# A different division of work between VectorE, ScalarE and GpSimd at three norms and in one attention of a fused transformer kernel

## What is computed

```python
h = _modulate(_rms_norm(x, g), shift, scale)     # h * (1 + scale) + shift
x = x + gate * _rms_norm(h_after_the_matrices, g_post)
```

```python
s = q . k * scale + mask            # 128 queries see themselves and up to 128 keys back
p = exp(s - max) / (sum(exp(s - max)) + exp(sink - max))
o = p . v
```

## Time and profile before

| | |
|---|---|
| median of 3 runs | 1689.22 us (1688.07 to 1692.46) |
| the profiled execution | 1697.89 us, of which the span is 1696.1 us |
| PE, PE weight load | 92% and 78% of the span |
| VectorE, ScalarE, GpSimd | 58%, 54% and 4% |
| norms that the diff touches | at about 366 to 384, 749 to 767 and 982 to 991 us of the span |
| the second attention | at about 1543 to 1625 us |

### The profile page before, as it was taken

One profiled execution on the slowest core, in us unless ns is written; L12 is line 12 of the kernel. 1 busy time (PEld: TensorE's weight loads), 2 busy tenths in 40 slices (PEclk: granted clock), 3 DMA queues, 4 the chain that ended last, 5 costly groups with the idle time before them and its releaser, 6 DMA issues.

```text
span 1696.1 us, 25703 instructions
## 1 busy us (share of the span) xinstructions
PE 1564.8 (92%) x10227; PEld 1315.7 (78%) x10227; DVE 984.4 (58%) x1602; ACT 918.0 (54%) x1518; POOL 63.3 (4%) x82
## 2 busy tenths in 40 slices
PE   5999898979999999979989989998999999888887
PEld 3777555748788888848845889998999999888777
DVE  2463666564343434464754676667766767577655
ACT  5653645464132323455555554556777867376745
POOL 3000032000000000000003000000000000000000
PEclk9999977989999999989986899999999999999899
DMA  7731535342433232342306366663635444343232
GB/s 245 222 99 50 174 100 174 119 129 75 149 100 99 91 102 82 113 143 75 124 13 207 118 197 191 197 199 128 227 127 173 150 150 141 109 133 117 91 108 75
DMA packets 223640, 225.40 MB, mean 133 GB/s; under 512 B 8234, under 2 KB 222064, under 8 KB 223472
## 3 DMA queue, kind: packets, MB, share of 16 engines
q1 hardware_dynamic: 222816, 223.63, 41.1%
q0 software_dynamic: 704, 0.12, 0.0%
HBM read 222.68 MB, written 1.05 MB: 132 GB/s over the span
## 4 chain that ended last, share of the span: by engine, by line
PE 73%; ACT 11%; DVE 11%; issue 2%; POOL 1%; DMA 0%; SPq 0%; DVEq 0%; ACTq 0%; POOLq 0%
PE bank L1039 20%; PE bank L1040 19%; PE bank L1041 19%; ACT SH L1701 2%; PE bank L1075 2%; ACT whi L1565 1%; DVE wlo L2116 1%; PE bank L1327 1%; PE bank L1060 1%; ACT H L1807 1%; PE bank L1234 1%; ACT HH L1807 1%; PE bank L1242 1%; PE bank L1349 1%; PE bank L1394 1%
## 5 line engine op out<-in xcount | busy, mean ns | idle before, releaser
L2116 DVE TENSOR_TENSOR wlo<-raw,whi 128x1024 fp32r<-128x1024 f32 (+2 forms) x322 | 387.9, 1208 | 259.0 <-ACT whi L1565 254.5
L1565 ACT ACTIVATE whi<-raw 128x1024 fp32r<-128x1024 f32 (+2 forms) x322 | 336.0, 1046 | 278.7 <-PE bank L1041 259.1
L1039 PE MATMUL bank<-HH,whi 128*128 128x512 f32 (+2 forms) x640 | 246.2, 385 | 22.1 <-DVE HL L2138 19.3
L1040 PE MATMUL bank<-HL,whi 128*128 128x512 f32 (+2 forms) x640 | 241.9, 378 | 0.0
L1041 PE MATMUL bank<-HH,wlo 128*128 128x512 f32 (+2 forms) x640 | 241.7, 378 | 0.0
L1039 PE MATMUL bank<-HA,whi 128*128 128x256 f32 x576 | 165.4, 287 | 13.7 <-DVE LA L2138 5.2
L1040 PE MATMUL bank<-LA,whi 128*128 128x256 f32 x576 | 162.3, 282 | 0.0
L1041 PE MATMUL bank<-HA,wlo 128*128 128x256 f32 x576 | 162.1, 281 | 0.0
L1039 PEld LDWEIGHTS bank<-HH,whi 128*128 128x128 f32 (+1 forms) x640 | 121.3, 190 | 50.8 <-issue 17.0
L1041 PEld LDWEIGHTS bank<-HH,wlo 128*128 128x128 f32 (+1 forms) x640 | 121.0, 189 | 23.6 <-issue 0.7
L1040 PEld LDWEIGHTS bank<-HL,whi 128*128 128x128 f32 (+1 forms) x640 | 121.5, 190 | 22.9 <-issue 1.2
(11 more groups left out here) (371 smaller groups left out, 3208.1 us busy)
## 6 DMA issues: line engine op xcount, KB each, us to landing
raw<-in_w_ff_dram SPq DMA_DIRECT2D x64, 1024.0 KB, 5.3
raw<-in_w_mod_dram SPq DMA_DIRECT2D x48, 1024.0 KB, 5.2
raw<-in_a_w_in_dram SPq DMA_DIRECT2D x40, 1024.0 KB, 5.0
raw<-in_w_in_dram SPq DMA_DIRECT2D x18, 1024.0 KB, 5.3
raw<-in_b_w_in_dram SPq DMA_DIRECT2D x9, 1024.0 KB, 5.3
raw<-in_w_out_dram SPq DMA_DIRECT2D x8, 1024.0 KB, 5.2
raw<-in_ple_w_gate_dram SPq DMA_DIRECT2D x8, 1024.0 KB, 5.1
raw<-in_a_w_out_dram SPq DMA_DIRECT2D x4, 1024.0 KB, 5.0
```

The costliest lines, as they stand in the source:

```text
L1039: nc.tensor.matmul(o, wh, xh, start=start, stop=False, skip_group_check=shared)
L1040: nc.tensor.matmul(o, wh, xl, start=False, stop=False, skip_group_check=shared)
L1565: f(whi[h % HALF_SLOTS][:, 0:n], raw[u.id % RAW_SLOTS][:, (h % 2) * n:(h % 2) * n + n], ACT.Copy)\
L2116: v.tensor_tensor(wlo[h % HALF_SLOTS][:, 0:n], raw[u.id % RAW_SLOTS][:, (h % 2) * n:(h % 2) * n + n], whi[h % HALF_SLOTS][:, 0:n].bitcast( ...
```

## The change

Four exponentials per pair that VectorE multiplied in `att2_scale` of the second attention are multiplied by GpSimd, as products of two tensors in which the inverse is broadcast along the columns; VectorE stops after the reciprocal and signals it (`s_p_inv`), and the transposes wait for GpSimd's signal (`s_p2_pool`). Layer 0's attention in the second block is as it was.

At the norms a table `h_by_dve` says for which tiles VectorE makes the full value. For 512 tokens these are k = 2, 4 and 6, except at the very first norm, which stays as it was; ScalarE then makes the high part of these tiles by one copy of the full value (128x512), and waits for it. For 256 tokens they are k = 0, 1, 3 and 5, and ScalarE makes the full values of 2, 4, 6 and 7 as well as all high parts.

```diff
+    h_by_dve = {True: (2, 4, 6), False: (0, 1, 3, 5)}
...
-            pe.wait_ge(s_p2, s_p2.at(ip))
+            if i == 0:
+                pe.wait_ge(s_p2, s_p2.at(ip))
+            else:
+                pe.wait_ge(s_p2_pool, s_p2_pool.at(ip))
...
+                first = (l, which) == (0, "mix")
+                by_dve = k in h_by_dve[t == ALL] and not first
+                if by_dve and t == ALL:
+                    act.wait_ge(s_h32, s_h32.at((l, which, k)))
+                    f(hi_part("h", l, which, k, slice(*t)), H32[n][:, k % 2, t[0]:t[1]], ACT.Copy).then_inc(*s_hh.tick((l, which, k)))
+                    continue
                 ops = [(hi_part("h", l, which, k, ts_), ts_, s) for s, ts_ in segs(t)]
-                if t == ALL:
+                if not by_dve:
...
-                if t != ALL:
-                    dve.wait_ge(s_xn, s_xn.at((l, "n", which, a_)))
-                    dve.wait_ge(s_fused, s_fused.at((l, which, a_ // 2)))
-                    for k in range(a_, b_):
-                        ins = v.tensor_scalar(H32[k // 2 % 2][:, k % 2, sl], XN[k // 2 % 2][:, k % 2, sl], fA[:, k, 0:1], modT[l][:, a + k, 0:1],
-                                              ALU.mult, ALU.add)
-                    ins.then_inc(*s_h32.tick(*((l, which, k) for k in range(a_, b_))))
+                for k in range(a_, b_):
+                    if k in by_dve:
+                        dve.wait_ge(s_xn, s_xn.at((l, "n", which, k)))
+                        dve.wait_ge(s_fused, s_fused.at((l, which, k // 2)))
+                        if k >= 4:
+                            dve.wait_ge(s_parts, s_parts.at((l, which, k - 4)))
+                        for s, ts_ in segs(t):
+                            ins = v.tensor_scalar(H32[k // 2 % 2][:, k % 2, ts_], XN[k // 2 % 2][:, k % 2, ts_], fA[:, k, 1 - s:2 - s],
+                                                  modT[l][:, a + k, 1 - s:2 - s], ALU.mult, ALU.add)
+                        ins.then_inc(*s_h32.tick((l, which, k)))
...
             if i == 1:
                 chain(v.tensor_tensor(small[:, total:total + 4], small[:, total:total + 4], small[:, sink:sink + 4], ALU.add))
+                v.reciprocal(small[:, inv:inv + 4], small[:, total:total + 4]).then_inc(*s_p_inv.tick(ip))
+                return
...
+            elif kind == "att2_second" and args[0][0] == 1:
+
+                ip = args[0]
+                pool.wait_ge(s_p_inv, s_p_inv.at(ip))
+                for e in (0, 1):
+                    for part, (a, n) in enumerate(((0, P), (P, SEQ))):
+                        c = att_col(ip, 3, e, part)
+                        p_ = att_p(ip, e)[:, a:a + n]
+                        ins = nc.gpsimd.tensor_tensor(p_, p_, bc(small[:, c:c + 1], [P, n]), ALU.mult)
+                ins.then_inc(*s_p2_pool.tick(ip))
```

More of the change, by code:

```diff
@@ L261, in build @@
     s_p2 = signal("p2")
+    s_p_inv = signal("p_inv")
+    s_p2_pool = signal("p2_pool")
     s_p_hi = signal("p_hi")
@@ L2385, in low @@
                 dve.wait_ge(s_hh, s_hh.at((l, which, b_ - 1)))
-                if t != ALL:
-                    dve.wait_ge(s_h32, s_h32.at((l, which, b_ - 1)))
+                for k in range(a_, b_):
+                    if k in by_dve:
+                        dve.wait_ge(s_h32, s_h32.at((l, which, k)))
                 (hi, lo), t0 = parts("h", l, which)
@@ L2391, in low @@
                      s_parts.tick(*((l, which, k) for k in range(a_, b_))))
+            by_dve = h_by_dve[t == ALL] if (l, which) != (0, "mix") else ()
             groups = [(0, 1), (1, 2), (2, 4), (4, 6), (6, 8)] if ups is None else [(k, k + 1) for k in range(*some)]
```

## The result

The changed kernel takes 1678.75 us (median of 9 executions, 1677.67 to 1684.28) where the kernel before, run beside it, takes 1692.46 (9 executions, 1688.07 to 1696.97). The ratio is 0.9927, with a 95% interval of 0.9912 to 0.9942: 12.4 us less, and 9.8 us at least (the two medians as they stand differ by 13.7). The forecast was 6.3 us less, 1683 us, with a range of 1678 to 1689. The kernel before does not repeat as well as the changed one: it lies between 1687.1 and 1699.1 us in all comparisons, its median was 1692.5, 1694.3, 1690.6 and 1689.9 in the four of them, and its profiled execution, 1697.89, is near the upper end. So the 19.4 us between the two profiled executions are no measure of the change.

The account below looks back on a forecast made before the run. PE, busy 92% of the span, was taken as the bound, so gains come only where it stands still. Terms 2.5 + 1.2 + 0.6 + 2.0 = 6.3 us, off the median of 1689.22: 1683 us, range 1678 to 1689.

Parts of the forecast that it names:

- The norm before layer 0's feed-forward part: Norm of 512 tokens: last low part starts 2.7 us earlier, PE finishes its wait for it 2.5 us earlier.
- The norm before layer 1's mixer: Norm of 512 tokens: PE late only by 0.7 us of the first wait and 0.49 of the last, gain 1.2 us.
- The norm of 256 tokens: VectorE loses four of eight full values, low parts come earlier, ScalarE's later last tile costs nothing: gain 0.6 us.
- The second attention: Chain gains 3.1 us at pairs 0, 1, 2, less 1.3 for locks, plus 0.2 at pair 7: 2.0 us.
- GpSimd's price: Second attention: GpSimd's four products put at 2.5 us a pair, between 2.3 and 4.2.
- the lock: VectorE and GpSimd block each other in the second attention: 0.3 us at each of three pairs, 0.4 once more.
- PE's loss at pair 1: Second attention: PE loses 0.7 us waiting for GpSimd, made up before the next two pairs' scores.
- Pair 7: Second attention: GpSimd's slower products and contention spend nearly all of VectorE's 1.04 us; 0.2 us remain.
- (a): Rival: the second attention gives nothing, locks and late transposes take back its 2.0 us; 1684.9 us, chance 0.22.
- (b): Rival: the norms' gain stays off PE's path, 1 to 2 us left of 4.3; 1686 us, chance 0.13.
- (c): Rival: slower, GpSimd's broadcast products take 4.2 us a pair, change loses from about 3.5; 1695.4 us, chance 0.07.
- (d): Rival: more than forecast, one stretch of low clock goes and pair 7 gains 1.04 us; 1680.5 us, chance 0.13.

Follow-up runs that it names:

- e6: Kernel before with only the norm before layer 1's mixer divided in the new way: 0.9971 of the kernel before, 4.9 us less.
- e12: Changed kernel, but VectorE does the four products itself at pairs 1 and 7 of the second attention: 1681.34 us, 0.9942 of the kernel before.
- e1: Kernel before with only the norms changed, second attention as before: 0.9927 of the kernel before, 12.4 us less.
- e11: Changed kernel measured again beside the kernel before, the second comparison: 1680.63 us beside 1689.94, ratio 0.9942.
- e2: Kernel before with only the second attention changed, all norms as before: 0.9983 of the kernel before, 2.9 us less.
- e4: Changed kernel with GpSimd's products per pair doubled, the added four into a tile nothing reads: 0.9947 of the kernel before.
- e13: As e12, but at norms of 512 tokens VectorE makes full values of tiles 0, 3, 5, 7: 1678.47 us, 0.9928 of the kernel before.
- e8: Kernel before with 14 products left out of layer 1's input projection, 3.2 us less work: 0.9994 of the kernel before, 1.0 us less.
- e9: Kernel before with 14 products done twice in layer 1's input projection, 3.2 us more work: 1.0017 of the kernel before, 2.9 us more.
- e5: Kernel before with only the norm before layer 0's feed-forward part divided in the new way: 0.9969 of the kernel before, 5.3 us less.

## Why the prediction was right, and where it was not

The direction and the mechanism were right: the gains that the traces show lie where PE waited for a low part or where VectorE's queue held the attention back. 1678.75 us lies in the range given, but only 0.75 us above its lower end. The size was too small, 6.3 us for 9.8 and 12.4. Term by term:

**The norm before layer 0's feed-forward part, 2.5 us.** Right. Up to the next norm the traces have 383.3 or 385.0 us before and 381.1 or 382.0 with the change, 2.2 to 3.0 less, and PE takes up the last two tiles 2.5 us earlier. The last low part is at 14.1 us as forecast (13.9 to 14.3), the copy at 0.63 (0.6 to 0.7), ScalarE's two waits at 0.76 and 0.75 (0.7 and 0.6), and the waits of 1.01 and 0.87 us are gone.

**The norm before layer 1's mixer, 1.2 us.** Too small by half; PE takes up the last two tiles 2.5 us earlier and the stage is 2.6 us shorter. The step that failed is "At layer 1 PE was late only by 0.7 of the first wait and by the 0.49 of the last": it took the gain to be what was left of the waits, with PE as slow between them as in that execution. But the last low part set PE's time in both executions of the kernel before, 17.21 us behind ScalarE's first instruction, with a wait of 0.49 in one and 0.85 in the other. e6 begins this norm just as the profiled execution of before did, with a first wait of 6.23 us; its next wait is 1.37 for 1.99, so 1.1 us of idle time are gone, about what the term says. Yet PE's second stretch of lower clock, 3.4 us long and 9.4 us behind ScalarE's first instruction in before, isn't there in e6, and PE takes up the last two tiles at 14.69. So the term kept a stretch of lower clock that did not stay. The schedule that gave 2.5 us at layer 0 would have given the same here. VectorE's timeline had already said so: from the first scaled tile to the last low part it has 16.7 us at both norms, and only PE was not alike.

**The norm of 256 tokens, 0.6 us.** The small waits removed are 0.66 us, and with the lower clock alike the gain is 0.1 to 0.6 us. The term stands at the upper end of this, and what the stage shows above it (1.2 to 2.4 us in six of seven traces) moves with a stretch of lower clock. That ScalarE's later last tile costs nothing was not quite right: PE waits 0.2 and 0.3 us for its low part in e12 and e1. The time shows 0.3 us (-1.7 to 2.5).

**The second attention, 2.0 us.** The part up to the later pairs was put at 1.8 (3.1 less 1.3 of locks), and the score product comes 1.8 us earlier in the traces of the changed kernel, of e11 and of e2. Two errors in it cancel, which is luck. GpSimd's price was 1.91 us a pair, below even the lower end (2.3): its products with one column broadcast take 0.40 and 0.61 us, where the sum had 0.45 and 0.72 from rows of two full tensors, and they follow each other without the gaps of 0.08. By e4 the mark moves by 3.4 us for 1.9 of price. And the lock was wider than put down: VectorE's small instructions beside GpSimd take 0.81 us for 0.36. The Trainium skill (SBUF — State Buffer, section Who interferes with whom) says just this, that a tensor-by-scalar instruction in a two-port mode is shut out as well, and these rows agree with it by 0.45 us at each of three pairs. They show the wait and not its cause, since these instructions also read their scalar from SBUF. By that rule the prediction would have had 0.8 us in place of 2.0; GpSimd was faster than the sum had it by 0.6 us a pair, which by e4 is worth 1.1. That PE's loss at pair 1 is made up was right (e12). Pair 7 was mis-sized: it was put at 0.2 us and brings 1.2 (e11 beside e12), since GpSimd takes 2.1 us there and VectorE comes to the gating of pair 6, on which PE's next product waits, without the four products in front. In all 3.0 us, and 2.9 by the times (e2).

**The rest.** Norms 2.6, 2.6 and 0.1 to 0.6 and attention 3.0 make 8.3 to 8.8 us by the stages. The fastest executions of the two kernels differ by 10.4 us in the first comparison and 7.8 in the second. The sum agrees with the second comparison (7.4 to 12.0 us less) and is below the first (9.8 to 14.9), whose kernel before stood 2.5 us higher than in the second and 3.2 above the median from which the forecast started. "PE's clock is in none of these terms" was said as a limit, and it is where the difference can lie, but no direct effect of the edit on it is shown. For one: in all nine traces in which the recurrence was reached earlier or later than by the kernel before, e13 apart, it took 83.3 to 84.9 us, with 87.5, 87.6 and 90.5 in three of the four where it was not. Against it: the fourth (e2) has 84.3, e13 has 87.1, and e8 and e9, which move nothing but the arrival, gain and lose by their times no more than their work. Their traces are no fair sample either: the profiled execution of e8 is the fastest of its twelve, those of e9 and e2 are the second fastest. What decides at which clock an execution passes the recurrence stays open, and so does whether the 1 to 4 us by which the two comparisons exceed the sum of the stages belong to the change.

**The rivals.** (a) falls by e2 and by the two marks in the attention, (b) by e5 and e6. (c) falls by the price, and by more than that: it had the change turn against itself from about 3.5 us a pair, and e4, at 3.8, is still 9 us faster than the kernel before. (d), more than forecast, is what came, and in part as it was put: pair 7 gains its 1.04 us and a little more. Its stretch of lower clock that goes as well is seen at the norm before layer 1's mixer (e6); in the attention no run shows one that goes with the edit.

## What to carry to other kernels

Do not price a gain by the length of a wait in one execution. Look for the time, counted from a fixed mark, at which the thing that you speed up lets the waiting engine go: here PE took up the last two tiles at 17.21 us in two executions whose waits were 0.49 and 0.85. A wait for a helper engine in the middle of a chain may cost nothing, even 1.9 us of it, if the next wait on the same engine shrinks by as much; compare the time between two marks across the stage, not the wait, and take the last mark behind the last place that the edit touches: a mark in the middle of the attention showed 1.8 of its 3.0 us. When two engines share tiles in pairs, give the helper the second tile of each pair, so that its result is there when the first engine comes to it (in e13 none of the copies waits); more came from handing over one of the two values that are made ahead of the first low part, on which everything waits (0.9 of 1.25 us).

## What the runs showed of the hardware

GpSimd multiplies 128 partitions by one broadcast column at 1.91 us for 768 columns in four instructions: 1.90 or 1.91 at seven of the eight pairs and 2.08 at the last, in the trace of the changed kernel, where its first product there starts beside VectorE's subtraction of two tensors and takes 0.57 us for 0.40. VectorE's instruction of 128 partitions by 2 columns waits for a whole instruction of GpSimd's: 0.68 us in place of 0.23. One program, the kernel before, passes the recurrence in 90.5 us at a granted clock of 0.77 in one execution and in 87.5 at 0.78 in another; e2, which issues the same work up to there, passes it in 84.3 at 0.87.
